# A two-layer decoder trunk: the expert value contraction with activations as the stationary operand

## The chip, the cores and the metric

One core of a Trainium2 chip. The metric is device time in microseconds of one launch; the time before is the median of 3 runs. The profile is one execution, recorded on the chip.

## The reference, cut to what matters

The kernel computes two layers for 256 tokens of width 1024. Each layer has a token mixer and then a layer of experts (PEER). The change lies in the last step of the experts: every token picks 8 x 16 of 16384 experts, and the value rows of those are summed with their coefficients.

```python
def peer_ffn(h, w_query, sub_keys, expert_u, expert_v):
    ...
        gate = jax.nn.softmax(best_s, axis=-1).astype(xb.dtype)
        u = expert_u[idx]
        v = expert_v[idx]
        act = jax.nn.gelu(jnp.einsum('nhkd,nd->nhk', u, xb), approximate=False)
        return jnp.einsum('nhk,nhkd->nd', gate * act, v)
...
        h = rmsnorm(x, ffn_norm_g[layer])
        x = x + peer_ffn(h, w_query[layer], sub_keys[layer], peer_u[layer], peer_v[layer])
    return rmsnorm(x, final_norm_g)
```

## The kernel before

The kernel doesn't gather. It computes the coefficient of every expert for every token, zero where an expert isn't picked, and holds it in `big` as 128 tiles of 128 experts x 256 tokens (`col(j)`, 128x256 each). The value stage (named `v0` and `v1` in `STREAM`) is then a dense product: 128 tiles of the value table, each 128 experts x 1024 columns (512 KB), contracted with the 128 coefficient tiles. Activations of the trunk lie transposed, model dimension on the partitions: `x` is 8 slices of 128x256.

The product is made nearly in full precision from single-pass fp32r matmuls: both operands are split in a high part and a rest, and three of the four products are summed. For each tile, in a ring of four buffers (`RAW`, index `r`):

- SyncE loads `raw[:, r]` from HBM once the rest of the tile four before is made (L328, waiting for `lo_dve`).
- ScalarE makes the high part `whi[:, r]` (L438), two tiles ahead and after the matmuls of the buffer's last user are done (`mm_done`), and then the high part of the coefficients `hhi[:, r]` (L675, signalled by `chi`).
- VectorE makes the rest `wlo[:, r]` (L1436), GpSimd the rest of the coefficients `hlo[:, r]` (L426, `clo`).
- TensorE waits for the four and issues 24 matmuls (L998, function `contract`): for each of 8 slices `m` of 128 columns of the value tile, (whi, hhi), (whi, hlo), (wlo, hhi). The slice of the value tile is the stationary operand, the 256 tokens stream past it. A matmul and its weight load are always one pair. The sums, 128 model columns x 256 tokens, lie in banks 4 to 7, two to a bank (`acc(m)`), and were set to zero before the stage (`clear`, L740).

When all 128 tiles are done, VectorE adds the four banks to `x` in four steps (`add_acc`, L1039, `x_done`). ScalarE squares each pair of slices (L471) and TensorE sums the squares over the partitions (`norm`, L747) in the bank that `norm_bank` names: bank 3, and bank 7 for norm number 3. The table for the square root is loaded by ScalarE (L567 after layer 0) ahead of its waiting for `x_done`. After layer 0 the second layer's mixer follows, with its first norm (number 2); after layer 1 the final norm (number 4) and the store.

TensorE's instructions run in the order written; the semaphores are written out by hand, with no planner.

Of the kernel before, what the change touches and what calls it, by code (L numbers as in the profile page):

```python
# [23 lines left out]
ALU = mybir.AluOpType  # L24
ACT = mybir.ActivationFunctionType
AX = mybir.AxisListType

P = 128
D = 1024
KC = D // P  # L30
T = 256
NB = T // P
# [21 lines left out]
FIRST, POOL_LO, DVE_LO = {}, {}, {}  # L54
# [10 lines left out]
COUNT = dict(STREAM)  # L65
# [23 lines left out]
def trunk(nc, x_t, par, con, w_dt, weights, sub_keys, out_t):  # L89
# [7 lines left out]
    def sem(name):  # L97
        return ctx.enter_context(nc.semaphore(name))

    with ctx:  # L100
        big = sb("big", [P, 128, T])
        raw = sb("raw", [P, RAW, KC, P])
        whi = sb("whi", [P, SPL, KC, P], F32R)
        wlo = sb("wlo", [P, SPL, KC, P], F32R)
        x = sb("x", [P, KC, T])
        hhi = sb("hhi", [P, KC, T], F32R)
        hlo = sb("hlo", [P, KC, T], F32R)
        pars = sb("pars", [P, NPAR])
        ident = sb("ident", [P, P])
# [14 lines left out]
        bank = [ctx.enter_context(nc.psum_tensor(f"bank{i}", [P, 512], F32)) for i in range(8)]  # L124
# [3 lines left out]
        def work(at, n, m=1):  # L128
            v = flat[:, at:at + n]
            return v if m == 1 else v.rearrange("p (m n) -> p m n", m=m)  # L130
# [5 lines left out]
        def acc(m):  # L136
            return bank[4 + m // 2][:, (m % 2) * T:(m % 2 + 1) * T]

        def norm_bank(n):
            return bank[7 if n == 3 else 3][:, 0:T]  # L140


        raw_in = [sem(f"raw_in{r}") for r in range(RAW)]
# [3 lines left out]
        mm_done = sem("mm_done")  # L147
# [16 lines left out]
        x_done = sem("x_done")  # L164
# [51 lines left out]
        obc = sem("obc")  # L216
        on = sem("on")

        sc_mm = sem("sc_mm")
        sc_a = sem("sc_a")  # L220
        tk = sem("tk")
# [48 lines left out]
        reset = work(24576, 2048, KC)  # L270
        sig = work(26624, 2048, KC)
        osquare = work(28672, 2048, KC)

        base = SCRATCH0 * T
        q_t = work(base, 4096, 2 * PH)
# [156 lines left out]
        def _(act):  # L432
# [89 lines left out]
            for q in range(HEADS // 2):  # L522
# [4 lines left out]
                if q % 4 == 3:  # L527
                    g = q // 4
                    for c in range(NB):
                        v = decay[:, c, 8 * g:8 * g + 8, :]  # L530
# [33 lines left out]
            for layer in range(2):  # L564
                if layer == 1:
# [32 lines left out]
                    n = len(LEVELS) + 1  # L598
# [24 lines left out]
                for n in range(2 * 4):  # L623
                    act.wait_ge(sc_mm, 8 * layer + n + 1)
                    b, m = divmod(n, 4)
# [51 lines left out]
                name = f"v{layer}"  # L677
# [3 lines left out]
                def v_round(i, end=False):  # L681
                    for r in range(RAW):
                        g = FIRST[name] + RAW * i + r
                        last = layer == 1
                        if not (end and r >= 2 and last):
                            hi(g + 2, (r + 2) % RAW)
                        if not (end and r >= 2):
                            act.wait_ge(mm_done, g + 2 - RAW + 1)
                            c_hi(RAW * i + r + 2, (r + 2) % RAW)
                with act.Fori(0, COUNT[name] // RAW - 1) as i:  # L690
                    v_round(i)
                v_round(COUNT[name] // RAW - 1, end=True)
            nc.scalar.preload_act_table(ACT.Sqrt)
            norm(4, x_done, range(9, 13))

        @block.tensor
        def _(pe):
# [45 lines left out]
            def norm(n):  # L743
                for k in range(KC):
                    if k % 2 == 0:
                        pe.wait_ge(sq_done, 4 * n + k // 2 + 1)
                    ins = nc.tensor.matmul(norm_bank(n), ones[:, :], sq[:, k, :], start=k == 0,  # L747
                                           stop=k == KC - 1)
                ins.then_inc(ms_done, 1)
# [7 lines left out]
            for k in range(KC):  # L757
                ins = nc.tensor.matmul(bank[4][0:HEADS, 0:T], wdt[:, k, :], hn[:, k, :], start=k == 0,
                                       stop=k == KC - 1)
# [5 lines left out]
            for n, (slot, c) in enumerate([(6, 0), (6, 1), (7, 0), (7, 1), (3, 0)]):  # L765
                ins = nc.tensor.transpose(bank[4][:, T + HEADS * n:T + HEADS * (n + 1)],
                                          small[0:HEADS, slot, c * P:(c + 1) * P], idn)
# [4 lines left out]
            for n in range(8):  # L772
                c, q = divmod(n, 4)
                b = (0, 1, 2, 3, 5, 6, 7, 0)[n]
                if n == 7:
                    pe.wait_ge(xt_v, 1)
                for m in range(4):
                    ins = nc.tensor.transpose(bank[b][:, P * m:P * (m + 1)],
                                              xc[:, 4 * q + m, c * P:(c + 1) * P], ident[:, :])
# [3 lines left out]
            for g in range(GROUPS):  # L783
                ins = nc.tensor.transpose(bank[4][:, P * g:P * (g + 1)], b_t[:, g, 0:P], ident[:, :])
            ins.then_inc(bt_mm, 1)
            for c in range(NB):
                pe.wait_ge(xt_v, 5 + c)
                for g in range(GROUPS):
                    t = slice(c * P, (c + 1) * P)
                    ins = nc.tensor.matmul(bank[5 + c][:, P * g:P * (g + 1)], b_t[:, g, t], c_t[:, g, t],  # L790
                                           start=True, stop=True)
# [3 lines left out]
            for q in range(HEADS // 2):  # L795
# [3 lines left out]
                for e in range(2):  # L799
                    h = 2 * q + e  # L800
                    ins = nc.tensor.matmul(bank[q % 4][:, e * T:(e + 1) * T],
                                           ident[0:HEADS, h:h + 1].to_broadcast([HEADS, P]),
                                           small[0:HEADS, 7, :], start=True, stop=True)
# [4 lines left out]
            for g in range(GROUPS):  # L808
                ins = nc.tensor.matmul(bank[4 + g][:, :], btok[:, g, :], xtail[:, 512 * g:512 * (g + 1)],
                                       start=True, stop=True)  # L810
# [51 lines left out]
            for layer in range(2):  # L862
                if layer == 1:
# [35 lines left out]
                    for n in range(4):  # L899
                        b, part = divmod(n, 2)  # L900
                        for m in range(4):
                            ins = nc.tensor.transpose(bank[n][:, P * m:P * (m + 1)],
                                                      ir[:, 4 * part + m, b * P:(b + 1) * P], ident[:, :])
# [8 lines left out]
                    for b in range(4):  # L912
                        for e in range(2):
                            h = 2 * b + e
                            v = slice(P * h, P * h + P)
# [4 lines left out]
                            ins = nc.tensor.matmul(o1, itok[:, 0, v], att2[:, h, :], start=False, stop=True)  # L920
# [3 lines left out]
                    for h in range(HGRN_HEADS):  # L924
                        if h % 2 == 0:
                            pe.wait_ge(osq, h // 2 + 1)
                        at = HGRN_HEADS - 1 - h
                        ins = nc.tensor.matmul(bank[4][0:HGRN_HEADS, 0:T], mean[:, at:at + HGRN_HEADS],
                                               osquare[:, h, :], start=h == 0, stop=h == HGRN_HEADS - 1)
                    ins.then_inc(oms, 1)  # L930
                    pe.wait_ge(orec, 1)
                    for h in range(HGRN_HEADS):
                        ins = nc.tensor.matmul(bank[4 + h // 2][:, (h % 2) * T:(h % 2 + 1) * T],
                                               ident[0:HGRN_HEADS, h:h + 1].to_broadcast([HGRN_HEADS, P]),
                                               oroot, start=True, stop=True)
# [10 lines left out]
                for n in range(8):  # L946
                    if n >= 4:
                        pe.wait_ge(sc_a, 8 * layer + n - 3)
                    b, q = divmod(n, 4)
                    for m in range(4):  # L950
                        ins = nc.tensor.matmul(bank[4 + n % 4][:, P * m:P * (m + 1)],
                                               q_t[:, 4 * q + m, b * P:(b + 1) * P], sk[:, 4 * q + m, :],
                                               start=True, stop=True)
# [4 lines left out]
                for n in range(6):  # L958
                    kind, b = divmod(n, 2)
                    if n == 4:  # L960
                        pe.wait_ge(gate_v, layer + 1)
                    ins = nc.tensor.transpose(bank[4 + n // 4][:, P * (n % 4):P * (n % 4 + 1)],
                                              lst[:, kind, b * P:(b + 1) * P], ident[:, :])
# [25 lines left out]
                name = f"v{layer}"  # L989

                def contract(i):
                    for r in range(RAW):
                        tile_ready(name, i, r)
                        pe.wait_ge(chi, 128 * layer + RAW * i + r + 1)
                        pe.wait_ge(clo, 128 * layer + RAW * i + r + 1)
                        for m in range(KC):
                            for w, h in ((whi, hhi), (whi, hlo), (wlo, hhi)):
                                ins = nc.tensor.matmul(acc(m), w[:, r, m, :], h[:, r, :], start=False,  # L998
                                                       stop=True, skip_group_check=True)
                        ins.then_inc(mm_done, 1)  # L1000
                with pe.Fori(0, 32) as i:
                    contract(i)
            norm(4)

        @block.vector
        def _(dve):
# [27 lines left out]
            def add_acc(value):  # L1034

                dve.wait_ge(mm_done, value)
                for b in range(4):
                    v = x[:, 2 * b:2 * b + 2, :]
                    nc.vector.tensor_tensor(v, v, bank[4 + b][:, :].rearrange("p (m t) -> p m t", m=2),  # L1039
                                            ALU.add).then_inc(x_done, 1)  # L1040
# [21 lines left out]
            v, u, w, t3, d, z, dt, acs = (sm(i) for i in range(8))  # L1062
# [36 lines left out]
            for i in range(CONV // 4):  # L1099
                dve.wait_ge(evac, 4 * i + 4)  # L1100
                for tap in range(4):
                    if tap:
                        dve.wait_ge(conv_step, 16 * i + 4 * tap)
                    for m in range(4 * i, 4 * i + 4):
                        src = pad[:, m, 3 - tap:3 - tap + T]
                        cw = par_at("conv_w", 4 * m + 3 - tap)
                        if tap == 0:
                            ins = nc.vector.tensor_scalar(xc[:, m, :], src, cw, par_at("conv_b", m),
                                                          ALU.mult, ALU.add)
                        else:  # L1110
                            ins = nc.vector.scalar_tensor_tensor(out=xc[:, m, :], in0=src, scalar=cw,
                                                                 in1=xc[:, m, :], op0=ALU.mult, op1=ALU.add)
# [6 lines left out]
            for n in range(8):  # L1119
                c, q = divmod(n, 4)  # L1120
                b = (0, 1, 2, 3, 5, 6, 7, 0)[n]
# [17 lines left out]
            for q in range(HEADS // 2):  # L1139
                dve.wait_ge(seg_mm, q + 1)  # L1140
                for e in range(2):
                    h = 2 * q + e
# [58 lines left out]
            for layer in range(2):  # L1201
# [231 lines left out]
                with dve.Fori(0, COUNT[name] // RAW) as i:  # L1433
                    for r in range(RAW):
                        dve.wait_ge(hi_done, FIRST[name] + RAW * i + r + 1)
                        nc.vector.tensor_tensor(wlo[:, r, :, :], raw[:, r, :, :], whi[:, r, :, :].bitcast(F32),  # L1436
                                                ALU.subtract).then_inc(lo_dve, 1)
                add_acc(FIRST[name] + COUNT[name])
            norm(4)


# [71 lines left out]
```

## Time and profile before

| | us |
|---|---|
| time, median of 3 runs (2453.83 to 2457.74) | 2456.57 |
| span of the profiled execution | 2450.6 |
| TensorE matmul busy | 2220.0 |
| GpSimd busy | 1483.6 |
| VectorE busy | 1228.8 |
| ScalarE busy | 1192.8 |
| value stages v0 and v1, first to last matmul | 2 x 368.9 |

How to read it: TensorE rows are given twice, PE for the matmul and PEld for the weight load, which overlaps the matmuls. Matmuls are pipelined, so the duration of one is longer than the time until the next can start; the rate is read from the starts, or from a chain piece divided by its count. The granted clock is a share of 2.4 GHz: 1.00 is that level, 0.50 is 1.2 GHz.

### The profile page before, as it was taken

The numbers are of one execution on the slowest core, as the hardware profiler recorded it, in microseconds if no ns is written. First come the engines' busy times: TensorE is split into PE (matmuls) and PEld (weight loads), VectorE is DVE, ScalarE is ACT, GpSimd is POOL, SyncE is SP. The second block draws the span as 40 slices with busy tenths as digits, with TensorE's granted clock in tenths as the row PEclk, the third lists the DMA queues.
The fourth block names the chain that finished last, engine by engine and source line by source line (L and its number), as shares of the span: only waits on it lengthen the run. The fifth ranks groups of instructions, "written<-read, shape, count | busy, mean of one in ns | idle before, by whom it ended". The sixth has DMA issues, their size and how long they took to land.

```text
span 2450.6 us, 49827 instructions
## 1 busy us (share of the span) xinstructions
PE 2220.0 (91%) x17350; PEld 2162.8 (88%) x17353; DVE 1228.8 (50%) x2068; ACT 1192.8 (49%) x1785; POOL 1483.6 (61%) x776
## 2 busy tenths in 40 slices
PE   6797899999996789999988888999999767999998
PEld 6796799999995689999988878999999656999998
DVE  3987429920009974444435641994000798444443
ACT  3444354445447754444445434544444676444443
POOL 4560579888885544444447436789888655444443
PEclk9997999999997789999999989999999878999999
DMA  4340445555550035555534224455555101555553
GB/s 153 129 137 18 141 149 168 178 177 175 180 186 2 0 112 182 184 182 181 182 126 153 95 86 137 146 180 171 174 182 182 45 0 61 183 185 180 181 185 105
DMA packets 94558, 341.27 MB, mean 139 GB/s; under 512 B 10416, under 2 KB 11952, under 8 KB 94128
## 3 DMA queue, kind: packets, MB, share of 16 engines
q1 hardware_dynamic: 94512, 340.67, 42.5%
q8 instruction: 27, 0.44, 0.1%
q14 instruction: 19, 0.16, 0.0%
HBM read 339.58 MB, written 1.05 MB: 139 GB/s over the span
## 4 chain that ended last, share of the span: by engine, by line
PE 45%; issue 27%; POOL 19%; DVE 8%; DVEq 1%; POOLq 0%; ACT 0%; ACTq 0%
PE bank L998 30%; POOL wlo L374 18%; PE bank L707 12%; DVE oha L1419 6%; PE bank L979 2%; DVE big L1408 1%; DVEq L1419 1%; PE bank L747 0%; DVE big L1021 0%; POOLq L378 0%; POOLq L373 0%; ACT whi L438 0%; DVE rstd L1019 0%; DVEq L1406 0%; DVEq L1427 0%
## 5 line engine op out<-in xcount | busy, mean ns | idle before, releaser
L374 POOL TENSOR_TENSOR wlo<-raw,whi 128x1024 fp32r<-128x1024 f32 x384 | 965.3, 2520 | 426.8 <-ACT whi L438 426.0
L707 PE MATMUL bank<-hhi,whi 128*128 128x256 f32 x3072 | 880.0, 286 | 76.4 <-DVE hlo L1031 33.6
L438 ACT ACTIVATE whi<-raw 128x1024 fp32r<-128x1024 f32 x640 | 674.9, 1055 | 421.6 <-PE bank L998 379.6
L707 PE MATMUL bank<-hlo,whi 128*128 128x256 f32 x3072 | 874.9, 285 | 0.0
L707 PE MATMUL bank<-hhi,wlo 128*128 128x256 f32 x3072 | 874.7, 285 | 0.0
L707 PEld LDWEIGHTS bank<-hhi,whi 128*128 128x128 f32 x3072 | 596.0, 194 | 84.1 <-issue 66.1
L707 PEld LDWEIGHTS bank<-hlo,whi 128*128 128x128 f32 x3072 | 596.1, 194 | 0.1
L707 PEld LDWEIGHTS bank<-hhi,wlo 128*128 128x128 f32 x3072 | 595.5, 194 | 0.0
L426 POOL TENSOR_TENSOR hlo<-big,hhi 128x256 fp32r<-128x256 f32 x256 | 352.5, 1378 | 388.6 <-ACT hhi L675 388.6
L998 PE MATMUL bank<-hhi,whi 128*128 128x256 f32 x2048 | 579.7, 283 | 3.5 <-POOL hlo L426 3.5
L998 PE MATMUL bank<-hlo,whi 128*128 128x256 f32 x2048 | 579.6, 283 | 0.0
L998 PE MATMUL bank<-hhi,wlo 128*128 128x256 f32 x2048 | 579.6, 283 | 0.0
L1436 DVE TENSOR_TENSOR wlo<-raw,whi 128x1024 fp32r<-128x1024 f32 x256 | 317.4, 1242 | 406.1 <-ACT whi L438 406.1
L998 PEld LDWEIGHTS bank<-hhi,whi 128*128 128x128 f32 x2048 | 393.2, 192 | 4.4 <-DVE wlo L1436 4.4
L998 PEld LDWEIGHTS bank<-hhi,wlo 128*128 128x128 f32 x2048 | 393.2, 192 | 0.0
L998 PEld LDWEIGHTS bank<-hlo,whi 128*128 128x128 f32 x2048 | 393.2, 192 | 0.0
L1419 DVE TENSOR_SCALAR oha<-iota,picks 128x128 f32<-128x128 f32 x384 | 213.1, 608 | 182.8 <-ACT big L633 91.4
L633 ACT ACTIVATE big<-bank 128x256 f32 x256 | 98.5, 385 | 399.9 <-PE bank L707 399.5
L979 PE MATMUL bank<-hlo,oha 128*128 128x128 f32 x1024 | 203.6, 365 | 92.3 <-DVE oha L1419 81.9
L979 PEld LDWEIGHTS bank<-hlo,oha 128*128 128x128 f32 x1024 | 177.1, 261 | 118.8 <-issue 97.4
L411 POOL TENSOR_TENSOR hhi<-iota,fives 128x640 fp32r<-128x640 f32 x96 | 121.8, 1271 | 87.7 <-ACT oha L664 76.9
L461 ACT ACTIVATE big<-bank 128x256 f32 (+1 forms) x104 | 39.9, 384 | 174.4 <-PE bank L707 174.4
(204 smaller groups left out, 1552.0 us busy)
## 6 DMA issues: line engine op xcount, KB each, us to landing
raw<-w_u SPq DMA_DIRECT2D x256, 512.0 KB, 3.3
raw<-w_v SPq DMA_DIRECT2D x256, 512.0 KB, 3.3
raw<-w_ssd_in SPq DMA_DIRECT2D x40, 512.0 KB, 3.4
raw<-w_q SPq DMA_DIRECT2D x32, 512.0 KB, 3.4
raw<-w_hgrn_in SPq DMA_DIRECT2D x32, 512.0 KB, 3.3
raw<-w_ssd_out SPq DMA_DIRECT2D x16, 512.0 KB, 3.4
raw<-w_hgrn_out SPq DMA_DIRECT2D x8, 512.0 KB, 3.5
big<-keys SPq DMA_DIRECT2D x2, 1024.0 KB, 6.5
```

Of the source, the lines that this page charges most:

```text
L374: nc.gpsimd.tensor_tensor(wlo[:, r, :, :], raw[:, r, :, :], whi[:, r, :, :].bitcast(F32), ALU.subtract).then_inc(lo_pool, 1)
L411: nc.gpsimd.tensor_tensor(dif[q], iota[:, :].unsqueeze(1).to_broadcast([P, 5, P]), fives[:, bass.ds(n, 1), :].rearrange("p a b -> p (a b)" ...
L426: nc.gpsimd.tensor_tensor(hlo[:, r, :], big[:, bass.ds(j, 1), :].rearrange("p a b -> p (a b)"), hhi[:, r, :].bitcast(F32), ALU.subtract).t ...
L438: nc.scalar.activation(whi[:, r, :, :], raw[:, r, :, :], ACT.Copy).then_inc(hi_done, 1)
L461: nc.scalar.activation(dst(t), bank[r][:, 0:T], ACT.Copy).then_inc(evac, 1)
L633: nc.scalar.activation(col(t), bank[r][:, 0:T], ACT.Gelu).then_inc(evac, 1)
L707: ins = nc.tensor.matmul(out, w[:, r, k, :], h[:, k, :], start=start and n == 0, stop=stop and n == 3 * KC - 1, **kw)
L979: ins = nc.tensor.matmul(bank[q][:, P * t:P * (t + 1)], oha[:, q % 2, t, :], ohb[q][:, t, :].bitcast(F32), start=True, stop=True)
L998: ins = nc.tensor.matmul(acc(m), w[:, r, m, :], h[:, r, :], start=False, stop=True, skip_group_check=True)
L1408: nc.vector.tensor_tensor(v, v, bank[b][:, :].rearrange("p (n j) -> p j n", n=4), ALU.mult).then_inc(gated, 1)
L1419: ins = nc.vector.tensor_scalar(oha[:, q % 2, t, :], iota[:, :], picks[:, 0, bass.ds(n, 1)], picks[:, 1, bass.ds(n, 1)], ALU.is_equal, ALU ...
L1436: nc.vector.tensor_tensor(wlo[:, r, :, :], raw[:, r, :, :], whi[:, r, :, :].bitcast(F32), ALU.subtract).then_inc(lo_dve, 1)
```

## The change

In the value stage the operands change roles. The coefficients of 128 tokens (`hhi` or `hlo`, a slice `tok` of 128 of the 256) become the stationary operand, and 512 columns of the value tile stream past. A tile takes 12 matmuls, 2 blocks of tokens x 3 products x 2 halves of the model dimension. The sums are now tokens x model dimension: bank 4 + 2b + e holds tokens of block b, columns 512e to 512e + 511. At the stage's end they are copied to `vt` in SBUF (a piece of `big` that is free by then), block 0 by VectorE and block 1 by ScalarE, two banks each; TensorE transposes the 16 blocks of 128x128 into banks 0 to 3, and VectorE adds these to `x` in four steps, each as soon as its group of four transposes is done. Norms 2 and 4 move from bank 3 to bank 7.

```diff
         def norm_bank(n):
-            return bank[7 if n == 3 else 3][:, 0:T]
+            return bank[3 if n < 2 else 7][:, 0:T]
...
+        vt_c = sem("vt_c")
+        vt_mm = sem("vt_mm")
...
+        vt = work(8192, 2048, NB)
...
                 v_round(COUNT[name] // RAW - 1, end=True)
+                act.wait_ge(mm_done, FIRST[name] + COUNT[name])
+                for e in range(2):
+                    ins = nc.scalar.activation(vt[:, 1, 512 * e:512 * (e + 1)], bank[6 + e][:, :], ACT.Copy)
+                ins.then_inc(vt_c, 1)
             nc.scalar.preload_act_table(ACT.Sqrt)
             norm(4, x_done, range(9, 13))
...
-                        for m in range(KC):
-                            for w, h in ((whi, hhi), (whi, hlo), (wlo, hhi)):
-                                ins = nc.tensor.matmul(acc(m), w[:, r, m, :], h[:, r, :], start=False,
-                                                       stop=True, skip_group_check=True)
+                        for b in range(NB):
+                            tok = slice(b * P, (b + 1) * P)
+                            for c, ws in ((hhi, (whi, wlo)), (hlo, (whi,))):
+                                for w in ws:
+                                    for e in range(2):
+                                        ins = nc.tensor.matmul(bank[4 + 2 * b + e][:, :], c[:, r, tok],
+                                                               w[:, r, 4 * e:4 * e + 4, :], start=False,
+                                                               stop=True, skip_group_check=True)
                         ins.then_inc(mm_done, 1)
                 with pe.Fori(0, 32) as i:
                     contract(i)
+
+                for b in range(NB):
+                    pe.wait_ge(vt_c, NB * layer + b + 1)
+                for n in range(4):
+                    for j in range(2):
+                        for b in range(NB):
+                            m = 2 * n + j
+                            ins = nc.tensor.transpose(bank[n][:, j * T + b * P:j * T + (b + 1) * P],
+                                                      vt[:, b, m * P:(m + 1) * P], ident[:, :])
+                    ins.then_inc(vt_mm, 1)
...
-                add_acc(FIRST[name] + COUNT[name])
+                dve.wait_ge(mm_done, FIRST[name] + COUNT[name])
+                for e in range(2):
+                    ins = nc.vector.tensor_copy(vt[:, 0, 512 * e:512 * (e + 1)], bank[4 + e][:, :])
+                ins.then_inc(vt_c, 1)
+                for n in range(4):
+                    dve.wait_ge(vt_mm, 4 * layer + n + 1)
+                    v = x[:, 2 * n:2 * n + 2, :]
+                    nc.vector.tensor_tensor(v, v, bank[n][:, :].rearrange("p (m t) -> p m t", m=2),
+                                            ALU.add).then_inc(x_done, 1)
```

## Rows read from the trace of the kernel before

**Rows 1.** A stretch of 350 us inside the first value stage, by engine.

```profile
core 0: us, PE busy (x) PEld busy (x) DVE busy (x) ACT busy (x) POOL busy (x), PEclk, DMA share, GB/s
900.00:1250.00 350.00, 350.00 (x2919) 350.00 (x2918) 147.72 (x121) 165.17 (x242) 168.13 (x122) 1.00 0.55 182
```

**Rows 2.** The chain of work through both value stages: start us, us, what.

```profile
886.49 368.88 PE bank L998 x3072
1255.37 0.02 issue
1255.39 0.70 DVE x L1039
...
1256.11 0.64 ACT big L471
...
2067.52 368.88 PE bank L998 x3072
```

**Rows 3.** Groups, 900 to 1250 us: busy us, mean ns, idle before and its releaser.

```profile
L426 POOL TENSOR_TENSOR hlo<-big,hhi 128x256 fp32r<-128x256 f32 x121 | 166.2, 1374 | 182.3 <-ACT hhi L675 182.3
L1436 DVE TENSOR_TENSOR wlo<-raw,whi 128x1024 fp32r<-128x1024 f32 x121 | 148.3, 1226 | 200.2 <-ACT whi L438 200.2
L438 ACT ACTIVATE whi<-raw 128x1024 fp32r<-128x1024 f32 x122 | 129.2, 1059 | 185.1 <-PE bank L998 185.1
L675 ACT ACTIVATE hhi<-big 128x256 fp32r (+1 forms) x120 | 48.1, 401 | 0.0
```

**Rows 4.** A stretch (columns as in rows 1) and timeline, TensorE at granted clock 0.50.

```profile
1268.00:1271.00 3.00, 3.00 (x15) 3.00 (x16) 0.85 (x1) 1.95 (x2) 0.96 (x1) 0.50 0.00 0
...
1268.35 0.41 PE L707 MATMUL bank<-hhi,wlo 128*128 128x256 f32 x1
...
1270.27 0.41 PE L707 MATMUL bank<-hhi,wlo 128*128 128x256 f32 x1
```

**Rows 5.** Timeline, TensorE, the same kind where a stream resumes, at full clock.

```profile
363.23 0.38 PE L707 MATMUL bank<-hhi,whi 128*128 128x256 f32 x1
363.45 0.28 PE L707 MATMUL bank<-hlo,whi 128*128 128x256 f32 x1
363.56 0.28 PE L707 MATMUL bank<-hhi,wlo 128*128 128x256 f32 x1
363.68 0.28 PE L707 MATMUL bank<-hhi,whi 128*128 128x256 f32 x1
```

**Rows 6.** Matmuls of 512 columns: bf16 (timeline; durations min/median/max), fp32 (its loads).

```profile
883.95 0.81 PE L740 MATMUL bank<-zero 128*128 128x512 bf16 x3
...
L740 PE MATMUL bank<-zero x9: 379/379/634, 234.6 to 2065.4; 128*128 128x512 bf16 x9
...
203.57 0.19 PEld L809 LDWEIGHTS bank<-big 128*128 128x128 f32 x1 [0.24 <-issue]
204.00 0.19 PEld L809 LDWEIGHTS bank<-big 128*128 128x128 f32 x1 [0.24 <-issue]
```

**Rows 7.** The page, DMA issues: the value tiles, KB each, us to landing.

```profile
raw<-w_v SPq DMA_DIRECT2D x256, 512.0 KB, 3.3
```

**Rows 8.** DMA from 888 to 900 us.

```profile
DMA packets 868, 3.17 MB, mean 265 GB/s; under 512 B 96, under 2 KB 96, under 8 KB 867
```

**Rows 9.** Timeline at the end of the first value stage.

```profile
1250.78 1.28 ACT L567 ACT_TABLE_LOAD   x1
...
1255.39 2.48 DVE L1039 TENSOR_TENSOR x<-x,bank 128x512 f32<-128x512 f32 x4 [9.14 <-PE bank L998]
```

**Rows 10.** Groups by form and timeline: copies of a bank, 16 transposes.

```profile
L1130 DVE COPY big<-bank 128x512 f32<-128x512 f32 x1 | 0.7, 680 | 0.0
...
L590 ACT ACTIVATE big<-bank 128x512 f32<-128x512 f32 x4 | 2.1, 602 | 0.7 <-PE bank L902 0.7
...
1383.04 1.97 PE L902 MATMUL bank<-ident,big 128*128 128x128 f32 x16 [0.47 <-ACT big L461]
...
L902 PE MATMUL bank<-ident,big x16: 272/272/328, 1383.0 to 1384.7; 128*128 128x128 f32 x16
```

## What the change does to the time, predicted

> **What bounds the kernel now.** The change touches only the two value stages, so I read those alone: the table of stretches first, then the chain, the groups with what they waited for, and only then single instructions.
>
> In a stretch of 350 us TensorE is busy all the time at a granted clock of 1.00, while VectorE has work for 148 us, ScalarE for 165 and GpSimd for 168, and the DMA engines are busy 55% [rows 1]. The chain gives each stage as one piece: 3072 matmuls in 368.88 us, with nothing between them [rows 2]. The groups show who waits for whom: VectorE and GpSimd sat idle for ScalarE's high parts (200 and 182 us of the 350), and ScalarE for the matmul of L998 (185 us), nobody for a transfer [rows 3]. So the stage is TensorE issuing matmuls back to back, and what counts is the distance from one start to the next: (368.88 - 0.28) / 3071 = 0.1200 us, 24 of them or 2.88 us a tile.
>
> **Where those 0.120 us go.** The 256 columns that a matmul streams take 256 / 2.4 = 106.7 ns at the higher clock level. 13.3 ns are left over, and the whole case hangs on what they are. Three observations: at the lower level the same kind of matmul starts every 0.213 us [rows 4], which is 256 / 1.2 = 213.3 and nothing more: an excess that went with each matmul would show there too (1268.35 to 1270.27 is 1.92 us for nine distances). Where one distance at full clock is stretched to 0.22 (363.23 to 363.45), so that the next load could be done ahead, the following one is 0.11, and only then it is 0.12 again [rows 5]. And where an instruction streams 512 columns with a load of its own before it, no excess of this size is seen: three bf16 matmuls 128x512 take 0.81 us, so with the last one's 0.379 as its length [rows 6] the distance is (0.81 - 0.379) / 2 = 0.2155; the fp32 matmuls of 512 columns have their weight loads 0.43 apart, two passes of 512, or 0.215 a pass [rows 6]. I read from this that a warm pair of 256 columns is limited by the weight load (128 columns into the array, one every 0.120), not by the columns, and that the load disappears behind a matmul that streams 213 ns.
>
> The Trainium skill speaks against so large a gain here. Its page "TensorE: Matmul & The Clock Gate", section "Back-to-back issue gap", puts the distance at N / 2.4 + 2.5 ns; by that 24 matmuls of 256 would take 2.62 us and 12 of 512 take 2.59, and the sum would be 8 us saved instead of 75. The row has 0.120 where that rule has 0.109, so for the 256-column pair the measurement decides and that sum has no chance of its own; for 512 columns rule (0.2158) and row (0.2155) agree.
>
> **The change, part by part.**
>
> *The contraction (L998).* 24 pairs of load and matmul with 256 columns become 12 pairs with 512. Columns streamed per tile are the same, 6144, as are tiles, semaphores, banks 4 to 7 and fp32r operands. No row shows fp32r with 512 columns. Bounds: 0.2133 (columns alone at 2.4 GHz) and 0.240 (two times the present distance). I take 0.2155, the rows with 512 columns [rows 6]; the row nearest in type is the 0.120 itself, but it is nearest where the load cannot hide. A stage is then 1535 x 0.2155 + 0.38 = 331.2 us instead of 368.9: 37.7 saved, 75.4 in both.
>
> *Does something else become the bound?* A tile would take 2.59 us instead of 2.88. Per tile ScalarE works 1.06 + 0.40, GpSimd 1.37, VectorE 1.23 [rows 3]. The loop that refills the splits: when tile j-2 is done, ScalarE splits tile j+2 (1.06) and its coefficients (0.40), GpSimd makes the low part (1.37): some 3.0 us with hand-overs, and the result is wanted after three tiles, 7.8 us. 4.8 us are to spare. The raw buffers: the low part by VectorE (1.23) frees one about 2.4 us after tile j-2, a transfer lands 3.3 us after it is issued [rows 7], sum 5.7, wanted after four tiles, 10.4. The queue itself moved 265 GB/s at the start of the stage [rows 8], 1.98 us a tile, and needs 202 GB/s. So nothing else comes up.
>
> *The end of a stage, added twice.* Before, VectorE adds bank 4 to x 0.02 us after the last matmul, and ScalarE squares it 0.70 later [rows 2]. Now the sums are turned first: VectorE copies two banks, ScalarE the other two, beside each other; TensorE makes 16 transposes in four groups; the four additions take place as before. Prices: a VectorE copy of 128x512 from a bank 0.68 [rows 10], a following one about 2.48 / 4 = 0.62 [rows 9], so 1.30; ScalarE 0.60 each [rows 10], 1.2, under it. The first group of four transposes: 16 of them took 1.97 us, each 0.27 long, so 0.113 apart [rows 10]: 3 x 0.113 + 0.27 = 0.61. Two hand-overs of 0.02 [rows 2] to 0.04. Sum 1.30 + 0.61 + 0.08 = 2.0 us a layer, all on the path. The other transposes (a group each 0.45) are under the additions (0.62 each). The last matmul's longer end is in the 0.38 above.
>
> What waits behind the new waits: on ScalarE the table load for the square root (1.28 us) was made at 1250.78, before the last matmul [rows 9]; now it stands behind the two copies, from 1.25 to 2.55 us after the end, and the first square is due at 2.0 + 0.70 = 2.7. It is hidden by 0.15 us; without that cover it costs up to 1.3. On TensorE the norm's matmuls stand behind the 12 remaining transposes: 1.35 us after the first group, against 0.70 + 0.64 for the first addition and square [rows 2]. Just level. If the clock falls to half during the idle 1.3 us and the transposes start 0.226 apart, the first group costs 0.3 to 0.4 more and the other twelve (2.7 us against 1.35) delay the norm by some 1.1 beyond that. The move of the second norm from bank 3 to bank 7 changes no duration. I take 4.0 us for both layers, from 3.4 (hand-overs of nothing and shorter copies) to 9.6 (2.0 + 1.3 + 1.5 in each). A gain here is excluded, as the added steps follow one another between the last matmul and the first addition.
>
> *Sum.* -75.4 + 4.0 = -71.4 us on the profiled 2450.6: 2379.2. The median of the runs shown is 2456.57, 6.0 above that span; the same 6.0 gives **2385.2 us**.
>
> **The rivals.**
>
> *A, the excess stays with each matmul of this type.* If the 13.3 ns are a cost of an fp32r matmul at the higher clock that the slower clock hides (a fixed part of a stage that is not slowed), the distance becomes 213.3 + 13.3 = 226.7 ns: 1535 x 0.2267 + 0.38 = 348.4, saving 20.5 a stage, 41.0 in all, less 4.0: 2419.6. For it: no fp32r row with other than 256 columns. Against it: the matmul that starts 0.11 after a stretched one [rows 5].
>
> *B, the time goes with the columns.* If streaming fp32r operands itself takes 0.120 per 256 columns, 12 of 0.240 are what 24 of 0.120 were, and only the end is added: 2460.6, within 0.2%. For it: 0.120 is so constant. Against it: the same 0.11 [rows 5], and that other operand types stream 512 columns in 0.2155.
>
> *C, slower: the granted clock is lost in the stage.* At 1.2 GHz 512 columns take 0.4267 us, 0.211 more than assumed; on all of a stage's 1536 matmuls that is 324 us, so each 1% of both stages costs 6.5 us. The gain of 71.4 is gone from 11% on; with a quarter of both stages it is 2385 + 162 = 2547 us. The place would be the stretches of the contraction that now stand at 1.00. For it: half as many instructions with longer ones between the events, and a longer pause at the layer's end. Against it: the engine has no pause within the stage before, and by my margins none after.
>
> *D, columns overlap.* If matmuls of 512 overlapped so far that TensorE was no bound, the transfer would be: 1.98 us a tile, 256 x (2.88 - 1.98) = 230 saved, 2230 with the end. No row has a column go faster than 2.4 per ns. The same section of the page named above reports 131 ns per matmul of 512 in a stream; by it a tile's matmuls would take 1.57 us, which is this rival, and the row with 0.2155 speaks against it.
>
> **How the numbers follow.** Forecast 0.78, A 0.11, B 0.06, C 0.04, D 0.01. The forecast's own range: 0.2133 and 3.4 us give 2456.6 - 82.2 + 3.4 = 2377.8; 0.216 and 9.6 give 2392. The lower end is 2377. As the forecast with its tails holds a little under 8 in 10, the range reaches up to A: 2420. A measurement of this kernel can tell about 0.2% (4.9 us) from no change. Faster by more: forecast, A and D, 0.90; within: B, 0.06; slower: C, 0.04.
>
> **What would show it.** In the profile after: 1536 matmuls of 128x512 in each stage, starting 0.215 to 0.216 apart, the stage in the chain at 331 us, the clock at 1.00, the transfer at about 202 GB/s, ScalarE, VectorE and GpSimd still waiting for the matmul. From the last matmul to the first addition about 2.0 us, the table load ended before the first square. It is wrong if the distance is 0.227 or 0.240, if the chain in the stage has pieces other than the matmul (then my margin of 4.8 us was misread), or if the first addition comes more than 3.5 us after the last matmul.

## The result, and the profile after

The median went from 2455.28 to 2420.40 us; the ratio is 0.9861, with a 95% interval from 0.9848 to 0.9873. So the kernel became faster by 34.9 us (1.4%, clear of the noise), where 71.4 were forecast. The time is that of rival A (2419.6), and lies just outside the range of 2377 to 2420.

The chain of the changed kernel, start us, us, what, at the end of the first value stage and for the second:

```profile
888.35 348.42 PE bank L1010 x1536
...
1236.79 1.30 DVE big L1463 x2
1238.09 0.14 issue
1238.23 0.64 PE bank L1023 x4
1238.89 0.70 DVE x L1468
1239.62 0.64 ACT big L476
1240.30 3.73 PE bank L756 x16
...
2051.02 348.42 PE bank L1010 x1536
```

L1010 is now the line of the contraction, L1463 the copies of the sums, L1023 the transposes, L1468 the additions. Each stage is still one piece, as in [rows 2], but of 348.42 us: (348.42 - 0.39) / 1535 = 0.2267 us from start to start, not 0.2155. A table of stretches inside both stages (us, busy us and instructions of PE, PEld, DVE, ACT, POOL, then clock, DMA share, GB/s):

```profile
900.00:1230.00 330.00, 330.00 (x1457) 273.27 (x1456) 148.34 (x121) 165.96 (x243) 166.58 (x122) 1.00 0.60 193
2065.00:2395.00 330.00, 330.00 (x1458) 273.34 (x1457) 147.11 (x120) 163.81 (x240) 164.21 (x121) 1.00 0.60 186
```

TensorE is busy throughout at full clock, as in [rows 1]. The weight loads no longer fill the time (273 of 330 us), so there is air between them, and yet the matmuls come no closer than 0.2267. In the same stage the others still wait, VectorE and GpSimd for ScalarE and ScalarE for the matmul (waits from 900 to 1200 us: total, times, longest):

```profile
DVE wlo L1459 <- ACT whi L443: 165.8, 111, 1.6
ACT whi L443 <- PE bank L1010: 150.3, 111, 1.4
POOL hlo L431 <- ACT hhi L680: 147.9, 110, 1.4
```

The whole difference of the two profiled spans, 2450.6 - 2415.7 = 34.9 us, can be laid out from the chains. Two stages give 2 x (368.88 - 348.42) = 40.9. From the end of the stage to the first addition it is 1238.89 - 1236.77 = 2.12 us where it was 0.02, and the same after the second stage: 4.2 together. The first stage began 1.9 us later (888.35 against 886.49), behind code that is the same in both, so this part is not the change's. 40.9 - 4.2 - 1.9 = 34.8.

### The profile page after: what moved, and what is told of

Same layout as the page of the kernel before. It is cut to its first block, busy times and chain, and to the rows that moved or that the text cites. A ratio compares the mean times of both kernels' runs of the same rounds, so it can differ in the third digit from the quotient of the medians.

```text
span 2415.7 us, 43760 instructions
## 1 busy us (share of the span) xinstructions
PE 2188.1 (91%) x14313; PEld 2010.4 (83%) x14313; DVE 1229.6 (51%) x2072; ACT 1195.4 (49%) x1789; POOL 1483.0 (61%) x776
## 4 chain that ended last, share of the span: by engine, by line
PE 44%; issue 27%; POOL 19%; DVE 8%; DVEq 1%; POOLq 0%; ACT 0%; ACTq 0%
PE bank L1010 29%; POOL wlo L379 19%; PE bank L716 12%; DVE oha L1442 6%; PE bank L988 2%; DVE big L1431 1%; DVEq L1442 1%; PE bank L756 0%; DVE big L1044 0%; POOLq L383 0%; POOLq L378 0%; ACT whi L443 0%; DVE rstd L1042 0%; DVEq L1429 0%; DVE big L1463 0%
## 5 line engine op out<-in xcount | busy, mean ns | idle before, releaser
L716 PE MATMUL bank<-hhi,whi 128*128 128x256 f32 x3072 | 880.6, 287 | 76.2 <-DVE hlo L1054 33.7
L716 PE MATMUL bank<-hlo,whi 128*128 128x256 f32 x3072 | 875.6, 285 | 0.0
L716 PE MATMUL bank<-hhi,wlo 128*128 128x256 f32 x3072 | 875.0, 285 | 0.0
L716 PEld LDWEIGHTS bank<-hhi,whi 128*128 128x128 f32 x3072 | 596.2, 194 | 84.1 <-issue 66.0
L716 PEld LDWEIGHTS bank<-hlo,whi 128*128 128x128 f32 x3072 | 596.4, 194 | 0.1
L716 PEld LDWEIGHTS bank<-hhi,wlo 128*128 128x128 f32 x3072 | 596.1, 194 | 0.0
L1010 PE MATMUL bank<-whi,hhi 128*128 128x512 f32 x1024 | 315.4, 389 | 3.5 <-POOL hlo L431 3.5
L1010 PE MATMUL bank<-wlo,hhi 128*128 128x512 f32 x1024 | 315.2, 389 | 0.0
L1010 PE MATMUL bank<-whi,hlo 128*128 128x512 f32 x1024 | 315.2, 389 | 0.0
L1010 PEld LDWEIGHTS bank<-whi,hhi 128*128 128x128 f32 x1024 | 192.1, 188 | 44.1 <-DVE wlo L1459 4.4
L1010 PEld LDWEIGHTS bank<-wlo,hhi 128*128 128x128 f32 x1024 | 192.2, 188 | 39.9
L1010 PEld LDWEIGHTS bank<-whi,hlo 128*128 128x128 f32 x1024 | 192.2, 188 | 39.9
```

Source lines behind the costliest of these rows:

```text
L716: ins = nc.tensor.matmul(out, w[:, r, k, :], h[:, k, :], start=start and n == 0, stop=stop and n == 3 * KC - 1, **kw)
L1010: ins = nc.tensor.matmul(bank[4 + 2 * b + e][:, :], c[:, r, tok], w[:, r, 4 * e:4 * e + 4, :], start=False, stop=True, skip_group_check=True)
```

## The experiments

The question is the 13.3 ns between a matmul's columns at 2.4 GHz and the distance to the next: the prediction took them for a weight load that doesn't hide behind 256 columns and would behind 512. The experiments with 256 columns and in fp16 were run 10 and 4 times, the others once; these are read by the distances in their traces, at the granted clock of the stage, which is 1.00 (900 to 1150 us) where nothing else is said.

**Width or role.** The change both swaps the operands and widens the stream. The first experiment keeps the swap and the new end, and goes back to 256 columns:

```diff
-                                    for e in range(2):
-                                        ins = nc.tensor.matmul(bank[4 + 2 * b + e][:, :], c[:, r, tok],
-                                                               w[:, r, 4 * e:4 * e + 4, :], start=False,
+                                    for e in range(4):
+                                        ins = nc.tensor.matmul(bank[4 + 2 * b + e // 2][:, (e % 2) * T:(e % 2 + 1) * T], c[:, r, tok],
+                                                               w[:, r, 2 * e:2 * e + 2, :], start=False,
```

> The roles are swapped as in the change (coefficients stationary, end of stage with copies and transposes), but each matmul streams 256 columns, so a tile has 24 of them. Theory now held (each fp32r matmul costs its columns at 2.4 GHz plus 13.3 ns, whichever operand is stationary): 0.120 us from start to start, stage 368.9 us, total that of the kernel before plus the added end, 2455.3 + 4.2 = 2459.5 us. Rival (the role of the operands matters, not the width): 0.1135 us a matmul, stage 348, total about 2420 us.

Measured 2459.29 us, ratio to the kernel before 1.0014 (1.0002 to 1.0027). Its chain (of the profiled run):

```profile
883.39 368.88 PE bank L1010 x3072
...
2073.10 368.88 PE bank L1010 x3072
```

That is the very 368.88 of the kernel before, with the other operand stationary. So the swap alone is worth nothing, its end costs 3.4 us in the medians (4.2 worked out from the chains above), and all of the gain comes from the width, through fewer matmuls. By the fixed excess, 1536 fewer a stage at 13.3 ns are 20.4 us, which is the 20.46 found.

**Another width.** 384 columns of each half instead of 512, a quarter of the model dimension left out:

```diff
-                                        ins = nc.tensor.matmul(bank[4 + 2 * b + e][:, :], c[:, r, tok],
-                                                               w[:, r, 4 * e:4 * e + 4, :], start=False,
+                                        ins = nc.tensor.matmul(bank[4 + 2 * b + e][:, 0:384], c[:, r, tok],
+                                                               w[:, r, 4 * e:4 * e + 3, :], start=False,
```

> As the changed kernel, but each matmul streams 384 columns: the last quarter of each half of the model dimension is left out. Fixed excess per matmul: 160.0 + 13.3 = 173.3 ns from start to start, total 2420.4 - 3072 x 0.0533 = 2256.6 us. Rival, excess grows with the columns (6.25% of 213.3): 170.0 ns, 2246 us. Rival, the excess is a step that comes with a full bank: 162.5 ns, 2223 us, where other work may bind.

Measured 2258.0 us, and the chain:

```profile
889.46 266.52 PE bank L1010 x1536
```

(266.52 - 0.33) / 1535 = 0.1734 us, that is 160.0 + 13.4 (0.33 is the length of the last matmul). Three widths now lie on one line: 120.0, 173.4 and 226.7 ns are 106.7, 160.0 and 213.3 plus 13.3 or 13.4. The theory of the prediction, that a load limits the pair to one in 0.120 us and disappears behind more columns, needs the excess to be gone at 160 ns of columns. It isn't.

**Less to load.** 64 stationary columns instead of 128, half of the tokens left out:

```diff
-                                        ins = nc.tensor.matmul(bank[4 + 2 * b + e][:, :], c[:, r, tok],
+                                        ins = nc.tensor.matmul(bank[4 + 2 * b + e][0:64, :], c[:, r, tok],
```

with `tok = slice(b * P, b * P + 64)`.

> As the changed kernel, but each stationary operand has 64 of a block's 128 tokens: half of the tokens are left out of the contraction, 512 columns stream as before. If the excess is a part of the weight load that does not hide and goes with its columns: about 220 ns from start to start, total 2400 us. If it belongs to the streaming, or is a fixed part of the load: 226.7 ns, 2420 us.

Measured 2428.0 us. Chain, and a group of its loads from 900 to 1200 us (busy us, mean ns); below it the same group of the changed kernel:

```profile
888.70 353.48 PE bank L1010 x1536
...
L1010 PEld LDWEIGHTS bank<-wlo,hhi 128*64 128x64 f32 x436 | 58.9, 135 | 42.3
...
L1010 PEld LDWEIGHTS bank<-wlo,hhi 128*128 128x128 f32 x440 | 82.6, 188 | 17.2
```

The load is shorter, 135 ns against 188, and the distance is longer, (353.48 - 0.39) / 1535 = 0.2300. Neither expectation has that: 0.220 is refuted, and 0.2267 is missed by 3.3 ns, for which I have no explanation. An excess that shrinks with the columns loaded is out.

**More pairs.** 128 columns, 48 matmuls a tile, the case in which a limit by the load would show undisguised:

```diff
-                                    for e in range(2):
-                                        ins = nc.tensor.matmul(bank[4 + 2 * b + e][:, :], c[:, r, tok],
-                                                               w[:, r, 4 * e:4 * e + 4, :], start=False,
+                                    for e in range(8):
+                                        ins = nc.tensor.matmul(bank[4 + 2 * b + e // 4][:, (e % 4) * P:(e % 4 + 1) * P], c[:, r, tok],
+                                                               w[:, r, e, :], start=False,
```

> As the changed kernel, but each matmul streams 128 columns, so a tile has 48. Fixed excess alone: 53.3 + 13.3 = 66.7 ns from start to start, 3.2 us a tile, total 2420.4 + 256 x (3.20 - 2.72) = 2543 us. Limit by the weight load, as the prediction had it (one every 0.120 us): 5.76 us a tile, total 3198 us.

Measured 3718.7 us, beyond both. Its two stages, in the chain and in stretches (us, then busy us and instructions of each engine, clock, DMA share and GB/s, as above):

```profile
885.27 686.28 PE bank L1010 x6144
...
2389.13 1309.65 PE bank L1010 x6144
...
900.00:1500.00 600.00, 600.00 (x5375) 600.00 (x5375) 137.21 (x112) 152.88 (x224) 153.48 (x112) 1.00 0.31 98
2410.00:3690.00 1280.00, 1280.00 (x6002) 1280.00 (x6002) 150.34 (x123) 166.08 (x244) 166.81 (x123) 0.50 0.15 49
```

In the first stage, at full clock, a pair comes every 686.28 / 6144 = 0.1117 us. That is closer than the 0.120 at which the prediction had the load as the limit, and each pair has its load (5375 and 5375), so 128x128 fp32r loads can follow each other faster than that. This takes away the mechanism, not only its size. The fixed excess fails here as well (66.7 was expected): at 128 columns the line doesn't hold, and 0.1117 and, at the lower clock, 1309.65 / 6144 = 0.2132 are about the time of 256 columns (106.7 plus 5, and 213.3). Whether 128 columns stream as if they were 256 or load and stream don't overlap at this width, the run doesn't tell. That the second stage ran at 0.50 is taken up below.

The kernel before has rows beside this. Its matmuls of L889 have plain fp32 operands (the views print f32 for fp32r as well), 128 columns and a load each:

```profile
1337.03 3.66 PEld L889 LDWEIGHTS bank<-big 128*128 128x128 f32 x32
1337.15 3.74 PE L889 MATMUL bank<-big 128*128 128x128 f32 x32
```

The loads, 0.19 long, start (3.66 - 0.19) / 31 = 0.112 us apart, and so do the matmuls. So 128x128 loads of four-byte operands closer than 0.120 stood in the trace from which the prediction was made, and with 128 columns an fp32r matmul takes no less than such an fp32 instruction.

**Which side of the matmul.** A bf16 matmul of zeros behind each fp32r one, to see at which kind of border the excess stands:

```diff
                                                                stop=True, skip_group_check=True)
+                                        ins = nc.tensor.matmul(bank[4 + 2 * b + e][:, :], zero[:, 0:P], zero[:, :],
+                                                               start=False, stop=True, skip_group_check=True)
```

> Behind every matmul of the contraction stands a bf16 matmul of zeros, 128x512, into the same bank. Two kinds of distance can then be read. Excess on the side of streaming fp32r: from an fp32r matmul to the zero one 226.7 ns, from the zero one to the next fp32r 215.5. Excess on the side of the fp32r weight load (not wholly hidden behind the matmul before it): the other way round, 215.5 and 226.7. Total the same by both: 2420.4 + 3072 x 0.2155 = 3082 us.

Measured 3136.7 us, 55 more than expected by either. The timeline:

```profile
999.59 0.58 PE L1010 MATMUL bank<-wlo,hhi 128*128 128x512 f32 x1
1000.01 0.39 PE L1013 MATMUL bank<-zero 128*128 128x512 bf16 x1
1000.05 0.58 PE L1010 MATMUL bank<-wlo,hhi 128*128 128x512 f32 x1
1000.47 0.39 PE L1013 MATMUL bank<-zero 128*128 128x512 bf16 x1
1000.51 0.58 PE L1010 MATMUL bank<-whi,hlo 128*128 128x512 f32 x1
```

The starts are 0.42 and 0.04 apart by turns, so the record of a start means another thing for the two kinds here, and by the ends (1000.17, 1000.40, 1000.63), which are modelled, both distances are 0.23. A pair takes 0.46 us, 18 ns more than 0.2267 + 0.2155 (54.7 us over the 3072 pairs). The experiment didn't answer its question. The 18 ns come with two changes of type; that the type is their cause is argued, not shown, though the other novelty, two matmuls running into the same bank, costs nothing in the kernel before, where six in a row do so at 0.120.

**The type.** Last, fp16 in place of fp32r for all operands that are split, in all stages, once in the changed kernel and once in the kernel before:

```diff
-        whi = sb("whi", [P, SPL, KC, P], F32R)
-        wlo = sb("wlo", [P, SPL, KC, P], F32R)
+        whi = sb("whi", [P, SPL, KC, P], F16)
+        wlo = sb("wlo", [P, SPL, KC, P], F16)
...
-        hhi = sb("hhi", [P, KC, T], F32R)
-        hlo = sb("hlo", [P, KC, T], F32R)
+        hhi = sb("hhi", [P, KC, T], F16)
+        hlo = sb("hlo", [P, KC, T], F16)
+        dbuf = sb("dbuf", [P, KC, T])
+        obuf = sb("obuf", [P, KC, T])
```

(`dbuf` and `obuf` take the fp32 scratch of the gates that lay in `hhi` and `hlo`. The operands' two parts then carry fp16's rounding instead of fp32r's; the computation is otherwise the same.)

> The changed kernel with fp16 in place of fp32r for all split operands of all stages. Theory (the 13.3 ns belong to the fp32r type): 0.2155 us in the value stages and 0.109 for 256 columns in the others. Value stages 3072 x 0.0112 = 34 us less; the other 9216 matmuls x 0.0108 = 100 us less unless GpSimd's low parts (2.52 us each, against 24 x 0.109 = 2.62) bind there; total 2286 us, up to 2320 where GpSimd binds. Rival (any matmul with a fresh 128x128 load in such a stream pays it): unchanged, 2420 us.

> The kernel before with fp16 in place of fp32r in all stages. Theory (excess belongs to the type): 0.109 us per matmul of 256 columns in the value stages too, 2.62 us a tile against 2.59 in the changed kernel with fp16. The change then loses its gain: 2286 + 256 x 0.03 - 4 = about 2290 us, no difference that counts. Rival (weight load limit of 0.120 for 256 columns whatever the type): 0.120 here and 0.2155 there, 75 us apart.

Measured 2295.1 us (ratio 0.9340, 0.9316 to 0.9363) with 512 columns and 2292.3 us (0.9337, 0.9311 to 0.9364) with 256. Both chains, the changed kernel's first:

```profile
842.43 331.69 PE bank L1012 x1536
```

```profile
833.50 335.53 PE bank L1000 x3072
```

With 512 columns the distance is (331.69 - 0.38) / 1535 = 0.2158, with 256 it is (335.53 - 0.27) / 3071 = 0.1092: the columns and 2.5 ns in both. So 10.8 of the 13.3 ns belong to the fp32r type. They may do so through the load as well as through the stream, since the type changes the load's record too, from 188 ns to 98 (changed kernel in fp16, 900 to 1150 us):

```profile
L1012 PEld LDWEIGHTS bank<-wlo,hhi 128*128 128x128 f16 x386 | 37.8, 98 | 45.5
```
 In the changed kernel the two value stages give 2 x (348.42 - 331.69) = 33.5 us of the 125.3, the other stages some 92 of the 100 expected of their 9216 matmuls. The stages differ by 3.8 us each, 7.7 together, of which the end takes 4.2 back; the medians are 2.7 us apart the other way, with intervals that overlap, so no difference is shown between the two. In fp16 the change is worth nothing that these runs can measure, and both beat the kernels of the case by 125 us or more.

**At the lower clock.** The prediction had argued that an excess going with each matmul should show at 1.2 GHz too. To see 512 fp32r columns there, VectorE was given needless work, so that TensorE idles:

```diff
+                        nc.vector.reciprocal(small[:, 2 * r:2 * r + 2, :],
+                                             raw[:, r, 0:4, :].rearrange("p (a b) k -> p a (b k)", a=2))
+                        nc.vector.reciprocal(oha[:, r // 2, 2 * (r % 2):2 * (r % 2) + 2, :], raw[:, r, 0:2, :])
                         nc.vector.tensor_tensor(wlo[:, r, :, :], raw[:, r, :, :], whi[:, r, :, :].bitcast(F32),
```

> The changed kernel with two needless reciprocals on VectorE ahead of each low part, 3.5 and 1.75 us, so that a tile takes VectorE some 6.5 us and TensorE (2.72 us of matmuls) idles in between; total about 2420 + 256 x (6.6 - 2.72) = 3413 us. It is to give rows of 512 fp32r columns at the lower clock level, if the granted clock falls. Theory (the 13.3 ns run beside a stream that is slow enough and show only at the higher level, as with 256 columns): 426.7 ns from start to start at 0.50. Rival (they are added at either level, and 256 columns at 0.50 are another case): 440 ns. If the clock stays at 1.00 it tells nothing, and 226.7 ns stand.

Measured 3252.0 us; 3413 was too much, as a tile took less than the 6.6 us assumed. The clock went up and down. A stretch at 0.50 (us, PE busy, clock, DMA) and its timeline:

```profile
903.90:906.40 2.50, 2.50 (x7) 0.50 0.44 167
...
903.93 1.06 PE L1010 MATMUL bank<-whi,hhi 128*128 128x512 f32 x2
904.79 1.06 PE L1010 MATMUL bank<-wlo,hhi 128*128 128x512 f32 x2
905.64 1.06 PE L1010 MATMUL bank<-whi,hlo 128*128 128x512 f32 x2
```

903.93 to 905.64 are four distances, 1.71 us: 512 / 1.2 = 426.7 ns each without any excess, where 440 would give 1.76. The excess that stands at 2.4 GHz at three widths is absent at 1.2 GHz. Its absence at the lower level therefore says nothing against it at the higher one.

## Why the prediction was wrong

**The bound.** Right: TensorE alone sets the stage, before and after, and nothing took its place. The transfers take 4.3 us to land instead of 3.3, which is 1.0 of the 4.7 us to spare by the prediction's sum (5.7 needed of 10.4).

**The distance at 512 columns.** This is the step that failed: "the load disappears behind a matmul that streams 213 ns", and with it the 0.2155. In its place the runs have, for fp32r with 256, 384 and 512 columns, the columns plus a fixed 13.3 ns (at 256 in either role), and so 0.2267. The term was sized at 37.7 us a stage and is 20.5; over both stages the error is 34.4 of the 35.2 us by which the median was missed. Rival A had the right mechanism and size (348.4 forecast, 348.42 found), and was given 0.11; its reason, a part that the slower clock doesn't slow, is not tested by any run.

Three observations had led to the load, and none of them carried it. The first, no excess at 1.2 GHz, is true and, by the last experiment, compatible with a fixed excess; rival A's own text had said how. The second, one distance of 0.11 after a stretched one [rows 5], was a single step at the border of a disturbance, read at a resolution of 0.01 us; the value 0.12 stood in thousands of distances. The third, 0.2155 with 512 columns [rows 6], was of bf16 and fp32, and turned out to be the law of another type: in fp16 the sum of the prediction, 331.2 us a stage, comes out at 331.69.

What was missing was a row of the same type at another width, and the kernel has none. The nearest row in type, 0.120, was set aside because it was thought to be bound by something else. With the bounds written down (0.2133 and 0.240), 0.2267 is the middle; nothing in the trace excluded it. A limit of one load in 0.120, on the other hand, was at odds with rows at hand: the loads of L889 above, 0.112 apart, and the prediction's own count for the 16 transposes, 0.113 [rows 10].

**The distance in fp16.** The Trainium skill, page "TensorE: Matmul & The Clock Gate", section "Back-to-back issue gap", puts the distance at N / 2.4 + 2.5 ns. The 0.120 that the prediction set against this rule decides for fp32r only. In fp16 the runs agree with the rule at both widths (109.2 and 215.8 ns by it; 0.1092 and 0.2158 us measured). By the same rule 12 matmuls of 512 instead of 24 of 256 save some 8 us over both stages, before the end is paid; in fp16 the two stages differ by 7.7.

**The end of the stage.** Right. 1.99 us had been worked out and 2.12 are in the chain: copies 1.30 (1.30), the first four transposes 0.64 (0.61), hand-overs 0.14 and 0.02 to 0.04 (0.08). The table load was behind the copies as forecast, and hidden, by 0.45 us instead of 0.15: ScalarE's two copies took 1.08 us together instead of 1.2, and the first square came 2.85 us after the last matmul instead of 2.7. The timeline of the changed kernel:

```profile
1236.79 1.08 ACT L700 ACTIVATE big<-bank 128x512 f32<-128x512 f32 x2 [4.32 <-PE bank L1010]
1236.79 1.29 DVE L1463 COPY big<-bank 128x512 f32<-128x512 f32 x2 [8.50 <-PE bank L1010]
1237.89 1.28 ACT L572 ACT_TABLE_LOAD   x1
1238.23 1.94 PE L1023 MATMUL bank<-ident,big 128*128 128x128 f32 x16 [1.47 <-DVE big L1463]
```

The remaining transposes were done at 1240.17, just before the norm's first matmul at 1240.30, as the "just level" had it.

**The other rivals.** B (time goes with the columns) is out by the three widths (it has 0.240 at 512), C (clock lost in the stage) by the 1.00 in both stages, D by 0.2267. What stays open is where in an fp32r matmul the 10.8 ns arise: on the side of the load or of the stream. Of the two experiments meant for it, one gave a refutation (it doesn't shrink with the columns loaded) and one no answer.

## What to carry to other kernels

A matmul costs its columns and a fixed part, and the fixed part depends on the type: 13.3 ns for fp32r (256 to 512 columns) and 2.5 for fp16 in this kernel's streams at 2.4 GHz, nothing that shows at 1.2 GHz for fp32r. Before widening matmuls, take the fixed part from rows of the same type, multiply it by the number of matmuls saved, and ask whether the type can be changed instead, at the price of its rounding; here that was worth 164 us (2456.8 to 2292.3) over all stages, 67 of them in the two value stages, and the widening 35. Swapping the operands to get the wider stream gains nothing by itself, and stays cheap where the sums, now turned, are turned back seldom: here 16 transposes for 128 tiles.

## What was not expected of the hardware

An engine that never paused ran nearly a whole stage at half clock. In the experiment with 128 columns both stages issue the same matmuls without a gap. The first was at 1.00 for 600 us and more, the second at 0.50 for 1280 us (rows above), and the time doubled with it, 0.1117 to 0.2132 us a pair. In both cases the engine had been working with short pauses before, and the clock stood at 1.00 when the stage began; in the second it fell just behind the start:

```profile
2380.00:2390.00 10.00, 6.77 (x48) 5.55 (x49) 8.43 (x18) 5.91 (x12) 2.10 (x2) 0.98 0.04 11
2390.00:2400.00 10.00, 10.00 (x51) 10.00 (x51) 4.00 (x4) 1.89 (x4) 4.14 (x4) 0.53 0.64 198
```

This was seen in one run, and what set the two stages apart is open. With 256 columns or more no value stage that ran without pauses was seen at the lower level. A comparison of kernels with such narrow fp32r matmuls can thus differ by a factor of two from one stage to the next for a cause that the code doesn't show.

With 64 stationary columns the distance grew by 3.3 ns, and bf16 and fp32r matmuls by turns took 18 ns a pair more than the two alone. Neither has an explanation here.
